# Constants awaited at their first use, pair order in a recurrent stage and full-height bias rows in a kernel of three chained blocks

## The reference, cut to what matters

```python
F = cumsum(log_sigmoid(f_pre))                 # forgetting attention
s = q @ k.T * scale + F[..., :, None] - F[..., None, :]
s = where(k_pos <= q_pos, s, -inf)
# mLSTM: D = b[t] - b[s] + i[s], m_t = running maximum, P = exp(D - m_t) * (q @ k.T)
```

## Time and profile before

| | |
|---|---|
| median of 3 runs | 4173.18 us (4168.72 to 4176.85) |
| the profiled execution's own time | 4174.3 us |
| its span | 4172.2 us |
| mean granted clock of TensorE | 0.911 |
| TensorE matmul busy | 3803.4 us, 91% |
| TensorE weight load busy | 3003.9 us, 72% |
| VectorE busy | 1366.2 us, 33% |
| ScalarE busy | 1218.4 us, 29% |
| GpSimd busy | 1293.5 us, 31% |

### The profile page before, as it was taken

One profiled execution on the slowest core, in us unless ns is written; L12 is line 12 of the kernel. 1 busy time (PEld: TensorE's weight loads), 2 busy tenths in 40 slices (PEclk: granted clock), 3 DMA queues, 4 the chain that ended last, 5 costly groups with the idle time before them and its releaser, 6 DMA issues. The chain is left out here.

```text
span 4172.2 us, 40010 instructions
## 1 busy us (share of the span) xinstructions
PE 3803.4 (91%) x16772; PEld 3003.9 (72%) x16772; DVE 1366.2 (33%) x2032; ACT 1218.4 (29%) x1787; POOL 1293.5 (31%) x531
## 2 busy tenths in 40 slices
PE   7869999999999999989978889999998989999987
PEld 6757688875676888755757777788777668757866
DVE  6953411133234212213452324201173231032342
ACT  4323322233233223322331112322234312223232
POOL 3523244442242444220420002344334214303432
PEclk9989999998899999878986778899999979979998
DMA  3212132221131232210220002222222102202231
GB/s 135 96 51 76 50 100 98 96 93 46 41 106 51 96 101 96 75 58 28 87 100 1 1 13 106 71 96 96 81 101 81 56 22 96 86 0 81 94 103 61
DMA packets 82812, 305.36 MB, mean 73 GB/s; under 512 B 8997, under 2 KB 10825, under 8 KB 81354
## 3 DMA queue, kind: packets, MB, share of 16 engines
q1 hardware_dynamic: 78368, 280.61, 20.3%
q10 hardware_dynamic: 4266, 22.21, 1.4%
HBM read 291.77 MB, written 11.02 MB: 73 GB/s over the span
## 5 line engine op out<-in xcount | busy, mean ns | idle before, releaser
L2383 POOL TENSOR_TENSOR WL<-RW,WH 128x1024 fp32r<-128x1024 f32 x527 | 1293.3, 2457 | 2846.3 <-ACT WH L261 2846.3
L266 PE MATMUL PS<-XH,WH 128*128 128x512 f32 x2968 | 1175.3, 396 | 105.0 <-POOL WL L2383 41.5
L267 PE MATMUL PS<-XL,WH 128*128 128x512 f32 x2968 | 1166.3, 393 | 0.0
L268 PE MATMUL PS<-XH,WL 128*128 128x512 f32 x2968 | 1165.4, 393 | 0.0
L261 ACT ACTIVATE WH<-RW 128x1024 fp32r<-128x1024 f32 x527 | 552.7, 1052 | 809.3 <-PE PS L268 658.1
L266 PEld LDWEIGHTS PS<-XH,WH 128*128 128x128 f32 x2968 | 564.5, 190 | 242.9 <-issue 53.6
L268 PEld LDWEIGHTS PS<-XH,WL 128*128 128x128 f32 x2968 | 563.8, 190 | 119.6
L267 PEld LDWEIGHTS PS<-XL,WH 128*128 128x128 f32 x2968 | 564.8, 190 | 116.2 <-issue 1.4
L266 PE MATMUL PS<-YH,WH 128*128 128x512 f32 (+1 forms) x928 | 352.6, 380 | 29.2 <-DVE YL L789 8.8
L267 PE MATMUL PS<-YL,WH 128*128 128x512 f32 (+1 forms) x928 | 351.1, 378 | 0.0
L268 PE MATMUL PS<-YH,WL 128*128 128x512 f32 (+1 forms) x928 | 350.8, 378 | 0.0
(11 more groups left out here) (425 smaller groups left out, 3703.1 us busy)
## 6 DMA issues: line engine op xcount, KB each, us to landing
RW<-in_units SPq DMA_DIRECT2D x527, 512.0 KB, 3.3
spill<-X ACTq DMA_DIRECT2D x2, 2048.0 KB, 6.9
X<-spill ACTq DMA_DIRECT2D x2, 2048.0 KB, 8.1
X<-in_xT SPq DMA_DIRECT2D x8, 256.0 KB, 6.6
A<-spill ACTq DMA_DIRECT2D x1, 2048.0 KB, 10.2
out_T<-X ACTq DMA_DIRECT2D x1, 2048.0 KB, 7.4
spill<-X ACTq DMA_DIRECT2D x1, 1536.0 KB, 5.1
spill_gates<-X ACTq DMA_DIRECT2D x1, 1536.0 KB, 6.0
```

What stands on the lines that cost most here:

```text
L266: mm(out, hi, xh, start=first, stop=False)
L267: mm(out, hi, xl, start=False, stop=False)
L268: return mm(out, lo, xh, start=False, stop=last)
L2383: nc.gpsimd.tensor_tensor(WL[:, u % SPLIT, :], RW[:, u % RAW, :], WH[:, u % SPLIT, :].bitcast(F32), ALU.subtract).then_inc(split_done, 1)
```

## The change

Four edits.

1. TensorE's wait for the constants goes from the head of its program into `rstd_pe`, and their load goes behind units 2 and 3.
2. In the recurrent stage the scores, the state product and y are issued in pairs of an even and an odd head, matmul by matmul, in place of head by head.
3. The far bias of the differential attention, the two bias rows of the mLSTM and that of the forgetting attention run over all 128 rows.
4. For that the tiles are cleared: four columns of `T(31)` ahead of their load, and `FL`, `GG` and `FX` at the head of `gif_take`.

```diff
             def rstd_pe(self, pe, st):
+                st.wait_ge(consts_in, 16)
                 st.wait_ge(*reached(f"{self.id}.sum"))
...
+        vs(lambda st: st.do(v.memset(T(31)[:, 0:4], 0.0), "rel.clear"))
         dma("onehot", T(30)[0:32, 0:384], io["onehot"], ready=["li.lo7"])
-        dma("rel", T(31)[0:32, 0:4], io["rel"])
+        dma("rel", T(31)[0:32, 0:4], io["rel"], ready=["rel.clear"])
...
-                mm(out[:, 0:(i - 1) * P], bcast(ident[0:32, 31:32], P), bcast(T(31)[0:32, h:h + 1], (i - 1) * P), start=False, stop=False)
+                mm(out[:, 0:(i - 1) * P], bcast(ident[:, 31:32], P), bcast(T(31)[:, h:h + 1], (i - 1) * P), start=False, stop=False)
...
-            for n, h in enumerate(heads):
-                j, b = h // 2, 64 * (h % 2)
-                c = slice(t * P, (t + 1) * P)
-                mm(PS[:, 6 * (h % 2), (n % 2) * P:(n % 2 + 1) * P], AR[j][b:b + 64, t, 0, :], T(j)[b:b + 64, c], start=True, stop=True)
...
+            c = slice(t * P, (t + 1) * P)
+            for q in range(2):
+                both = [(n, heads[n] // 2, 64 * (heads[n] % 2)) for n in (q, q + 2)]
+                for n, j, b in both:
+                    mm(PS[:, 6 * (b // 64), q * P:(q + 1) * P], AR[j][b:b + 64, t, 0, :], T(j)[b:b + 64, c], start=True, stop=True)
+                for n, j, b in both:
+                    mm(PS[:, 1 + n // 2, q * 256:(q + 1) * 256], T(j)[b:b + 64, c], AR[j][b:b + 64, t, :, :].rearrange("p w c -> p (w c)"), start=True, stop=True)
+                for n, j, b in both:
+                    mm(PS[:, 3 + n // 2, q * 256:(q + 1) * 256], T(30 + j)[b:b + 64, c], AR[j][b:b + 64, t, :, :].rearrange("p w c -> p (w c)"), start=True, stop=True)
...
-                for h in range(8):
...
+                for j in range(4):
+                    c = lambda b: slice(t * P + b, t * P + b + 64)
+                    o = lambda b: PS[b:b + 64, 7, j * 64:(j + 1) * 64]
+                    for b in (0, 64):
+                        mm(o(b), T(4 + j)[rows, c(b)], T(8 + j)[rows, c(b)], start=True, stop=False)
+                    if j == 0:
                         st.wait_ge(*reached(f"u{n}"))
+                    for q in range(2):
+                        last = mm(o(64 * q), T(18 + j)[rows, c(64 * q)], UT[rows, slot(2 * j + q), :], start=False, stop=True)
...
+            for j in range(4):
+                o = lambda b: PS[b:b + 64, 5, j * P:(j + 1) * P]
+                for q in range(2):
+                    mm(o(64 * q), UT[:, slot(2 * j + q), :], RB[:, slot(2 * j + q), 0, :], start=True, stop=False)
+                for q in range(2):
+                    mm(o(64 * q), T(8 + j)[:, t * P + 64 * q:t * P + 64 * q + 64], RB[:, slot(2 * j + q), 1, :], start=False, stop=False)
                 for cc in range(2):
+                    for b in (0, 64):
+                        last = mm(o(b)[:, 64 * cc:64 * cc + 64], ST[(2 * t + cc) % 3][b:b + 64, j * 64:(j + 1) * 64],
+                                  AR[j][b:b + 64, t, 1, 64 * cc:64 * cc + 64], start=False, stop=(cc == 1))
...
         def gif_take(st):
+            for x in (FL, GG, FX):
+                st.do(v.memset(x, 0.0))
+            st.settle()
             st.wait_ge(*reached("tn.r"))
...
-                mm(o, bcast(ident[0:4, h:h + 1], P), GG[0:4, c0:S], start=True, stop=False)
+                mm(o, bcast(ident[:, h:h + 1], P), GG[:, c0:S], start=True, stop=False)
...
-                    st.do(mm(PS[:, 7, :], bcast(ident[0:4, h:h + 1], P), FL[0:4, :], start=True, stop=True), f"ml.m{h}")
+                    st.do(mm(PS[:, 7, :], bcast(ident[:, h:h + 1], P), FL[:, :], start=True, stop=True), f"ml.m{h}")
...
-            mm(out, bcast(ident[0:8, h:h + 1], P), FX[0:8, 0:(i + 1) * P], start=False, stop=False)
+            mm(out, bcast(ident[:, h:h + 1], P), FX[:, 0:(i + 1) * P], start=False, stop=False)
...
-            sp.dma_start(CST[:], io["consts"]).then_inc(consts_in, 16)
             for j in range(2, RAW):
                 sp.dma_start(RW[:, j, :], w[:, j, :]).then_inc(raw_full[j], 16)
+            sp.dma_start(CST[:], io["consts"]).then_inc(consts_in, 16)
...
         def _(pe):
-            pe.wait_ge(consts_in, 16)
             walk("tensor", pe, tensor_steps)
```

More of the change, by code:

```diff
@@ L1780, in scores_pe @@
             st.wait_ge(*reached("p1.turned11"))
-            for n, h in enumerate(heads):
-                j, b = h // 2, 64 * (h % 2)
-                c = slice(t * P, (t + 1) * P)
-                mm(PS[:, 6 * (h % 2), (n % 2) * P:(n % 2 + 1) * P], AR[j][b:b + 64, t, 0, :], T(j)[b:b + 64, c], start=True, stop=True)
-                mm(PS[:, 1 + n // 2, (n % 2) * 256:(n % 2 + 1) * 256], T(j)[b:b + 64, c], AR[j][b:b + 64, t, :, :].rearrange("p w c -> p (w c)"), start=True, stop=True)
-                last = mm(PS[:, 3 + n // 2, (n % 2) * 256:(n % 2 + 1) * 256], T(30 + j)[b:b + 64, c], AR[j][b:b + 64, t, :, :].rearrange("p w c -> p (w c)"), start=True, stop=True)
+            c = slice(t * P, (t + 1) * P)
[7 more added lines that the diff above has]
+                    mm(PS[:, 3 + n // 2, q * 256:(q + 1) * 256], T(30 + j)[b:b + 64, c], AR[j][b:b + 64, t, :, :].rearrange("p w c -> p (w c)"), start=True, stop=True)
             for q in range(2):
@@ L1929, in state_pe @@
                 st.do(last, f"u.mm{n}")
-                for h in range(8):
[L1931 to L1935, removed]
+                for j in range(4):
[4 more added lines that the diff above has]
+                    if j == 0:
                         st.wait_ge(*reached(f"u{n}"))
-                    last = mm(o, T(18 + j)[rows, c], UT[rows, slot(h), :], start=False, stop=True)
+                    for q in range(2):
+                        last = mm(o(64 * q), T(18 + j)[rows, c(64 * q)], UT[rows, slot(2 * j + q), :], start=False, stop=True)
                 st.do(last, f"s.mm{n}")
[L1939 to L1943, removed]
+            for j in range(4):
[4 more added lines that the diff above has]
+                    mm(o(64 * q), T(8 + j)[:, t * P + 64 * q:t * P + 64 * q + 64], RB[:, slot(2 * j + q), 1, :], start=False, stop=False)
                 for cc in range(2):
-                    last = mm(o[:, 64 * cc:64 * cc + 64], ST[(2 * t + cc) % 3][b:b + 64, j * 64:(j + 1) * 64],
-                              AR[j][b:b + 64, t, 1, 64 * cc:64 * cc + 64], start=False, stop=(cc == 1))
+                    for b in (0, 64):
+                        last = mm(o(b)[:, 64 * cc:64 * cc + 64], ST[(2 * t + cc) % 3][b:b + 64, j * 64:(j + 1) * 64],
+                                  AR[j][b:b + 64, t, 1, 64 * cc:64 * cc + 64], start=False, stop=(cc == 1))
             st.do(last, f"y.mm{t}")
```

## The result

The changed kernel takes 4058.3 us (median of four runs, 4055.0 to 4059.2) against 4172.7 before: a ratio of 0.9724 with a 95% interval of 0.9707 to 0.9741, 114 us faster.

The account below looks back on a forecast made before the run. It took TensorE, busy but at half clock under matmuls using few rows, as the bound. Terms summing to 90.6 us plus 5 for clock, 95.6 from 4174.3, gave 4078.7; the forecast was 4078 us, range 4035 to 4118.

Parts of the forecast that it names:

- The scores' order: Recurrent scores: alternating heads on different row halves takes 4.60 us a group in place of 7.29; 18.8 us saved.
- y's order: Recurrent y: paired heads on different column halves overlap, 6.6 us saved in each of four chunks; 26.4 us.
- the clock term: Recurrent stage: denser work may lift the clock in part of y and the scores; 5 us, between 0 and 15.
- The rival in which L1945's pairs stay serial: Last step of y: pairs writing one PSUM bank don't overlap; 7 us less saved, 4085 (14%, with a 4102 form).
- The forgetting attention: Its full-height bias rows save shape changes and keep the clock; 31 us saved, bounds 15 and 36.
- The mLSTM: Its 16 full-height bias rows save shape changes and halve the cold stretch; 10.9 us saved, bounds 5.9 and 13.
- The differential attention: Its 16 full-height bias rows save shape changes, 4 us in all; the cold stretch was expected to stay.
- More clock: Differential attention leaves 0.50 early, about 25 us, and recurrent chunks run at full clock, 10 more: 4043 us; 18%.
- The clearing: Zeroing three tiles on VectorE ahead of its convolution costs 1.5 us, all of it counting.
- The start: Program start: TensorE no longer waits for the constants, so the variance product comes earlier; 1.0 us saved, bounds -1 and 1.3.
- The first rival: Full-height bias rows bring no clock, only waits and shapes gain: 26 us less saved, 4104 us; 15%.
- Slower by alternation: Recurrent scores and y: each alternation drains the array, 0.29 us at half clock, nothing overlaps; 8 us slower, 4182; 3%.

Follow-up runs that it names:

- fillers: Changed kernel plus six unused 256-column products in each recurrent group wait and mLSTM head wait: 4045.2 us over 128 rows, 4047.0 over 64, 4064.8 over 8.

## Why the prediction was right, and where its sizes were off

The mechanism held in the two stages that carry the gain, not at the start, and in the mLSTM it isn't shown. The terms of the sum, against the table of stages:

**The scores' order**, 18.8 forecast. Right for the order, and low for the clock: a pair takes 2.29 us at half clock, a group 4.57 (4.60 forecast), and the scores alone brought 22.9. The group behind the transfer, left out of the sum, has nothing to give; the three behind a y, in which the clock came back, gave 4.91 each, the other four about 2.7 to 3.0. (A head of scores is 6 records, not 12, and four heads have three boundaries, two of them serial; neither enters the sum.)

**y's order**, 26.4 forecast, at the upper bound; y gained 30.6 over the four chunks. The pairs overlap fully at half clock, 1.67 us as forecast, and the 4.2 above the forecast are clock that comes back inside y. The mis-sized term is the clock term, 5 us taken between 0 and 15. It came to about 11: these 4.2, and 4.57 - 2.38 = 2.2 in each of the three score groups behind a y, 6.6 (the first group is at full clock before, too). With 45.2 and these 10.8 the stage should gain 56.0; it gained 61.3, and the gate products behind it 2.3 more, which now begin at full clock and which no term held. The timelines place the rest, but for rounding: 3.0 between the second group's masked products and y, 0.8 of it the state product, forecast at nothing; 1.9 around the masking; and 0.5 in the score groups. I had put the 5 near its lower end "because before nothing under this pattern was lifted". That was no evidence about the pairs: before, the row halves took turns, and the pairs keep both at work. That this is what brought the clock back in y was not tried by itself: in the recurrent waits fillers over 64 rows did nearly as much as those over 128, and the pairs fill both column halves of the array as well.

**The rival in which L1945's pairs stay serial** (14% with its larger form) fell. The rows: eight records of L1953 in 0.62 us (2234.34 to 2234.96), where four of the old order take the same 0.62 (2238.91 to 2239.53 in the kernel with only the scores in pairs). By the rule of the Trainium skill (TensorEngine Tiling, Gotcha 1: PSUM Pressure) the two row halves writing one bank would have been in each other's way; these, in different partitions of bank 5, were not.

**The forgetting attention**, 31 forecast with 36 as bound; 36.9 came, 0.9 beyond the bound. The step that failed was "I expect some falls in the 2 us wait to remain and take 11.0". None remained: 10.18 per head, the 10.2 worked out for full clock. The shape change at 0.39 was right as a price (12.5 of the whole), and the clock was the larger part, as the extra 8-column products show.

**The mLSTM**, 10.9 forecast, 11.8 from its first to its last product. That the number fits is in part luck. The stage takes 91.6 us in the profiled execution of before, but 87.9 to 88.1 in the four other kernels whose rows are low here; with the full-height rows it takes 79.8 to 81.9, the kernels with fillers apart. So the edit is worth 6 to 12 us, and this pair of traces lies at the upper end. The lower end is the 5.9 of the shape changes alone; that the full-height spread row counts as dense work, the guess behind the other 5, is not shown. The long cold stretch of some 6.8 us at a waiting head does get rarer with the edit, but is not gone: the kernel with the full-height rows alone has one.

**The differential attention**, 4 forecast, 3.5 in the changed kernel and 4.7 with the rows alone. The clock stayed at 0.50 for its first 66 us; its 64-row matmuls remain.

**More clock** (18%, 4043) came half true, and the time lies between it and my own case: the recurrence gained 11.1 more than forecast, where the rival has 10; its other half, 25 us in the differential attention, did not come.

**The clearing**, -1.5 forecast. It cost 1.7 by the new wait at L266 for L2082, and about 2.5 by the stretch from y to the mLSTM, in the kernels that differ in little else (773.4 us against 771.0 with the pairs alone). The place was named wrongly: the wait of 7.4 behind the convolution is still 7.4; TensorE waits for `gif_take` itself, in which the clearing now stands first.

**The start**, 1.0 forecast. Nothing: -0.2 at 982 here, none with the constants alone. The step that failed was to price the gain at the variance product and to let it run on from there. Already that product came at 23.33, not at the 22.7 forecast, its sum being ready later. Behind it TensorE still waits 20 us for GpSimd's weights and 7 to 8 for VectorE; neither had been moved.

**Not forecast**: 3.2 us in the block attention, whose code is the same. The kernel with only the scores in pairs has it too (78.8 us there, 81.9 to 82.0 in the others); the clock comes back earlier in some executions. And 2.1 us in the stretches between the stages and the tail. Together: 11.1 (recurrence, 61.3 against 50.2) + 2.3 + 5.9 + 0.9 - 0.5 - 0.2 - 1.2 + 3.2 + 2.1 = 23.6, by which 119.2 exceeds 95.6.

**The first rival**, that the height brings no clock (15%), fell in the forgetting attention and in the fillers. Its argument was that the first heads were as busy as can be. They were, at 18.79 of 20 us, and cold. The Trainium skill's account (TensorE: Matmul & The Clock Gate, What's actually happening), by which busyness sets the clock, differs from these rows: busier windows over few rows are cold, less busy ones over 128 rows are not. **Slower by alternation** fell as well: a pair takes no more than a head did.

## What to carry to other kernels

Where TensorE is busy and its granted clock is still 0.50, look at how many rows its matmuls use before looking at the gaps: give small matmuls (bias rows, masks, broadcasts) all 128 rows with zeros, and issue two half-height ones of different halves next to each other. Price such a change at the stage behind it as well, since the clock it brings back lasts into the next products. An engine that starts earlier gains nothing unless the one it waits for next also does.

## What the runs showed of the hardware that I had not expected

- The clock goes by rows in use, by degrees: fillers over 128 rows kept it at the mLSTM heads (spread row 1.12 us), over 64 at one of three (1.12, 1.82, 2.05, one execution), over 8 at none (2.07), at the same busy time. How many of the array's columns they use made no difference (recurrent stage 264.5 against 264.3 us).
- Changes of array shape take time but hardly any clock: 32 tiny products of another shape cost 17.3 us, some 0.5 each, and the windows behind the first head stay at 1.00.
- Unused work made the kernel faster: six products in each of eight group waits and three head waits, and 11 to 13 us came off.
- Pairs on opposite row halves overlap wholly even where they write one PSUM bank: eight records in the 0.62 us of four.
- The same serial score group takes 7.29 or 3.78 us by what ran before it.
